# The second norm's weight is multiplied in on VectorE after the gathered rows are transposed

## The chip, the cores and the metric

The kernel runs on one core of one Trainium2 chip. The metric is the device time of one execution in microseconds (us). The kernel before took 1095.0 us as the median of three runs (1093.69 to 1096.15 us).

## The reference, cut to what matters

One decoder layer works on 544 tokens of width 1024: 512 of a prompt and 32 of eight sample sequences.

```
xn = rms_norm(x, mix_norm_g)
h  = x + mixer(xn)                      # three gated branches, three projections, one output projection
hn = rms_norm(h, ffn_norm_g)            # h * rsqrt(mean(h*h) + eps) * ffn_norm_g
group  = argmax(softmax(hn @ w_group + b_group))           # 1 of 4
top 2  of the 8 experts of that group, by hn @ w_router + b_router
y  = h + sum over the 2 experts of gate * (silu(hn @ w_gate_e) * (hn @ w_up_e)) @ w_down_e
out = rms_norm(y, final_norm_g)
```

There are 32 experts with three weight matrices of 1024 x 512 in float32, 2048 KB each, so 6 MB an expert. All of them are read. The change concerns `ffn_norm_g`, the weight of the second norm, 1024 numbers: each row of `hn` is multiplied by it, element by element.

## The kernel before, in words

Everything is float32, and every instruction is placed by hand on one of five queues: SP issues the transfers, TensorE (PE) multiplies and transposes, ScalarE (ACT), VectorE (DVE) and GpSimd (POOL) do the rest. They wait for each other through semaphores. The order of each queue is the order of its text.

**The mixer** fills the time to about 517 us. Its weights come in blocks of 1024 x 256 through two buffers (`wring`, lines 474 to 476); ACT writes the high part of each block (`high_part`, line 885), POOL subtracts it to get the low part (`low_part`, line 1445), and PE multiplies both (lines 587 and 628). At the start SP issues the inputs, 32 tiny pieces of the gating weights (line 437) and eight "late" loads (lines 439 to 450), and only then the third weight block. Near the end of the mixer SP reloads `x` and loads `ffn_row`: `ffn_norm_g` repeated on all 128 partitions (line 473).

**The second norm and the routing** (about 517 to 563 us). The rows of `h` lie in `x`, 128 tokens a chunk, five chunks (the last has 32 rows). PE transposes them (line 770) and multiplies by the router's weights (line 757); those weights were multiplied by `ffn_norm_g` on DVE at the start (line 1118), and each row's scale is applied to the logits later (line 1275), so the routing needs neither the scaled rows nor the weight row. ACT scales the rows into `xn2` (line 1035, one instruction for a chunk, semaphore `h_scaled`). POOL multiplies each chunk of `xn2` by `ffn_row` in place (line 1509, semaphore `xn2_done`), SP stores the chunk to DRAM as `xn2_dram` (lines 494 to 497, semaphore `xn2_stored`). Meanwhile DVE computes the routing from the logits, one small instruction after the other (lines 1289 to 1366), with two exponentials on ACT (lines 1038 and 1040) and three small products on PE (lines 786, 787 and 792). It ends with a table of row numbers, `block_rows`, and the semaphore `routed`.

**The experts.** For each expert, POOL copies a column of row numbers (line 1517) and gathers 64 token rows as 128 half rows of 512 from `xn2_dram` with an indirect transfer (line 1520, `gather`). It waits for `routed` and for all of `xn2_stored` first. PE transposes the half rows into PSUM (`turn_rows`, line 803), DVE copies the 128 x 512 result to SBUF as `xgT` (`take_rows`, line 1372), and PE multiplies by the gate and up matrices (`gate_up`, line 814). ACT applies silu (line 1046), DVE multiplies (`times_up`, line 1378), PE transposes (line 825), ACT copies (line 1052), PE multiplies by the down matrix (`down`, line 835), ACT copies the result out (line 1058), and POOL scatters it (line 1532). PE's order is written out: gate/up of e, transposing of the rows of e+1, transposing of the hidden values of e, down of e.

**The weight stream.** Gate/up matrices have three places, down matrices three; the third place of each is used once, for expert 2. SP's order from 517 us on: gate and up of expert 0, up and down of expert 1 (gate of 1 and down of 0 came earlier), the five stores of `xn2`, down of expert 2 (line 499, into `late_rows`, where `ffn_row` lay), then a wait for all stores and for the first two gathers (lines 500 to 502), gate and up of expert 2, and then for each later expert (`load_expert`, line 506): wait until the gate/up product two experts earlier is done, load gate and up, wait for the down product, load down. `final_row`, the weight of the last norm, lies where `ffn_row` lay; both loads count on `norm_rows_loaded`.

Of the kernel before, what the change touches and what calls it, by code (L numbers as in the profile page):

```python
# [22 lines left out]
P = 128  # L23
D = 1024
# [8 lines left out]
NCH = SEQ // P + 1  # L33
# [5 lines left out]
CAP = 64  # L39
# [10 lines left out]
def chunk_rows(c):  # L50
    return P if c < NCH - 1 else NS
# [47 lines left out]
def build(nc, d, out):  # L99
    ctx = ExitStack()  # L100
    with ctx:
        program(nc, d, out, ctx)


def program(nc, d, out, ctx):
    def sb(name, shape, dt=F32):
        return ctx.enter_context(nc.sbuf_tensor(name, shape, dt))
# [8 lines left out]
    def sem(name):  # L116
        return ctx.enter_context(nc.semaphore(name))
# [22 lines left out]
    gate_of = sb("gate_of", [P, 2, NCH])  # L140
    block_rows = sb("block_rows", [P, 2 * NBLK], I32)
    idx_now = sb("idx_now", [P, 4], I32)
    ovf = sb("ovf", [P, NOVF + 1], I32)
    ps = ctx.enter_context(nc.psum_tensor("ps", [P, 8, 512], F32))

# [22 lines left out]
    late_rows = xx[:, KD * T:]  # L168
# [14 lines left out]
    pool_hist = row_a[:, 0:KW * NSEQ * PH].rearrange("p (q t) -> p q t", t=NSEQ * PH)  # L183
    xT = xx[:, 0:KD * T].rearrange("p (k t) -> p k t", t=T)

    ffn_row = final_row = late_rows[:, 0:D]
    pool_d = mid[:, 0:KW * T].rearrange("p (q t) -> p q t", t=T)
    vn = mid[:, KW * T:KW * T + NCH * W].rearrange("p (c n) -> p c n", n=W)
    merged = mid[:, 0:KD * T].rearrange("p (q t) -> p q t", t=T)
# [10 lines left out]
    xn2 = flat_y[:, 0:NCH * D].rearrange("p (c n) -> p c n", n=D)  # L200
# [19 lines left out]
    xgT = [work[:, SPARE + 4 * D + s * 512:][:, 0:512].rearrange("p (c m) -> p c m", c=4) for s in range(2)]  # L220
# [16 lines left out]
    def halves(v):  # L237
        return v.rearrange("p (b n) -> p b n", b=2)
# [7 lines left out]
    def halves_at(t, q):  # L246

        return t[:, bass.ds(q, 1)].rearrange("p a (b n) -> p (a b) n", b=2)
# [34 lines left out]
    rows_loaded = sem("rows_loaded")  # L283
    late_loaded = sem("late_loaded")
    norm_rows_loaded = sem("norm_rows_loaded")
    high_ready = sem("high_ready")
    low_ready = sem("low_ready")
    step_loaded = sem("step_loaded")
# [31 lines left out]
    conv_high = sem("conv_high")  # L320
    conv_low = sem("conv_low")
    tap_step = sem("tap_step")
    xn2_done = sem("xn2_done")
    rstd_in = sem("rstd_in")
    h_scaled = sem("h_scaled")
    xn2_stored = sem("xn2_stored")
# [14 lines left out]
    xgT_ready = sem("xgT_ready")  # L341
# [75 lines left out]
    def _(sp):  # L417
# [17 lines left out]
        for b in range(NSEQ):  # L435
# [10 lines left out]
            (router_b[:, 0:NG], d["b_group"][0].partition_broadcast(P)),  # L446
            (router_b[:, NG:], d["b_router"][0].partition_broadcast(P)),
        ]
        for dst, src in late:
            sp.dma_start(dst, src).then_inc(late_loaded, 16)  # L450

# [3 lines left out]
        for n in range(2, len(pairs)):  # L455
            if n == FIRST_D1 + 2:

                sp.wait_ge(v_normed, NCH)
                sp.dma_start(out["chunk_v_sample"][0].rearrange("b i c -> (b i) c"), vn[0:NS, NCH - 1]).then_inc(outs_stored, 16)
                sp.wait_ge(act_took, A_G0 + 2)  # L460
                sp.dma_start(out["pool_prompt"][0][0], states[0:PH, 0]).then_inc(states_stored, 16)
                sp.dma_start(out["conv_prompt"][0][0], states[0:CH, 2]).then_inc(states_stored, 16)
                for b in range(NSEQ):
                    r = slice(b * STEP, (b + 1) * STEP)
                    sp.dma_start(out["pool_sample"][0][b, PH - STEP:PH], states[r, 1]).then_inc(states_stored, 16)
                    sp.dma_start(out["conv_sample"][0][b, CH - STEP:CH], states[r, 3]).then_inc(states_stored, 16)
            if n == FIRST_OUT + 2:


                sp.wait_ge(merged_done, KD)  # L470
                sp.dma_start(x[:, 0:4], d["x_prompt"][0].rearrange("(c p) n -> p c n", p=P)).then_inc(x_again, 16)
                sp.dma_start(x[0:NS, 4], d["x_sample"].rearrange("b i n -> (b i) n")).then_inc(x_again, 16)
                sp.dma_start(ffn_row, d["ffn_norm_g"][0].partition_broadcast(P)).then_inc(norm_rows_loaded, 16)
            sp.wait_ge(low_ready, n - 1)
            rows = pairs[n].rearrange("(k p) n -> p k n", p=P)
            sp.dma_start(wring[n % 2][:, 0:rows.shape[1]], rows).then_inc(wring_loaded[n % 2], 16)
# [15 lines left out]
        load_down(1, 1)  # L492

        for c in range(NCH):
            sp.wait_ge(xn2_done, c + 1)
            n = chunk_rows(c)
            sp.dma_start(xn2_dram[c * P:c * P + n], xn2[0:n, c]).then_inc(xn2_stored, 16)

# [35 lines left out]
        for c in (4, 0, 1, 2, 3):  # L534
            n = chunk_rows(c)
            sp.dma_start(y_place(c)[0:n], y_rows[c * P:c * P + n]).then_inc(y_loaded[c], 16)
        for i, c in enumerate(FINAL_ORDER):
            sp.wait_ge(final_done, i + 1)
            n = chunk_rows(c)
# [543 lines left out]
    def _(dve):  # L1083
        v = nc.vector
        n_own = [0]

        def own(instruction):

            n_own[0] += 1
            instruction.then_inc(dve_step, 1)  # L1090
            dve.wait_ge(dve_step, n_own[0])
# [9 lines left out]
        for c in range(NCH):  # L1101
            n = chunk_rows(c)
# [49 lines left out]
        for c in range(NCH):  # L1152
            n = chunk_rows(c)
# [7 lines left out]
        for c in range(NCH):  # L1161
            n = chunk_rows(c)
# [70 lines left out]
        with dve.Fori(0, NJ // 2) as i:  # L1233
            for b in range(4):
                m = halves_at(merged, i * 4 + b)
                t = halves(tmp[b % 2][:, 0:T])
# [12 lines left out]
        for i in range(2):  # L1249
            for c in range(NCH):  # L1250
                n = chunk_rows(c)
# [20 lines left out]
        for c in range(NCH):  # L1272
            n = chunk_rows(c)
# [94 lines left out]
        def take_rows(e, s, turn, free):  # L1368
            dve.wait_ge(xg_turned, e + 1)
            if free is not None:  # L1370
                dve.wait_ge(gu_done, free)
            v.tensor_copy(xgT[s].rearrange("p c m -> p (c m)"), ps[:, s]).then_inc(xgT_ready, 1)  # L1372

        def times_up(e, s, turn, free):
            dve.wait_ge(sig_ready, e + 1)
# [2 lines left out]
            v.tensor_tensor(hid[s], sig[s], ps[:, 2 + s, 256:512], ALU.mult).then_inc(hid_ready, 1)  # L1378

        dve.wait_ge(xn2_stored, 16 * NCH)  # L1380
        take_rows(0, 0, 0, None)
        for e in range(2):
            take_rows(e + 1, 1 - e, e, None if e == 0 else 1)
            times_up(e, e, 0, None)
        with dve.Fori(1, NE // 2 - 1) as i:
            for s in range(2):
                take_rows(2 * i + s + 1, 1 - s, i + s, 2 * i + s)
                times_up(2 * i + s, s, i, 2 * i + s - 1)
# [9 lines left out]


        own(v.memset(stat[:, 95:96], EPS))  # L1400
        dve.wait_ge(norm_rows_loaded, 32)

        def last_sum(c):
            dve.wait_ge(y_loaded[c], 16)
# [22 lines left out]
    def _(pool):  # L1427
        g = nc.gpsimd
# [73 lines left out]
            low_part(s, FIRST_OUT + 2 + s)  # L1502


        pool.wait_ge(norm_rows_loaded, 16)
        for c in range(NCH):
            n = chunk_rows(c)
            pool.wait_ge(h_scaled, c + 1)
            g.tensor_tensor(xn2[0:n, c], xn2[0:n, c], ffn_row[0:n], ALU.mult).then_inc(xn2_done, 1)

        def gather(e, s, turn, free):
# [77 lines left out]
```

## Time and profile before

| what | value |
| --- | --- |
| median of three runs | 1095.0 us (1093.69 to 1096.15) |
| span of the profiled execution, first to last instruction | 1089.4 us |
| own time of the profiled execution | not listed apart from its span; the median lies 5.6 us above the span |
| busy share of the span | PE 79%, PEld 54%, DVE 36%, POOL 30%, ACT 18% |
| read from HBM, written | 256.60 MB, 13.74 MB |

How to read it: an engine's busy share is an average over very different stretches. The page also has a strip that cuts the span into 40 slices of 27.2 us, with busy tenths for each engine, the clock that TensorE was granted, and what the transfers moved. The chain of waits follows the work back from the last instruction: at each step to what released it, or to the instruction before it on its engine. A line number (L1372) is a line of the kernel. SPq is SP's queue of transfers.

### The profile page before, as it was taken

To read this page: it belongs to the slowest core of one execution; us is meant where nothing else is said; L and a number is where in the kernel's file an instruction comes from. 1 tells how busy PE (TensorE), PEld (TensorE's weight loads), DVE (VectorE), ACT (ScalarE), POOL (GpSimd) and SP (SyncE) were. 2 spreads that over 40 slices of the span, in tenths; PEclk is the share of its full clock that TensorE was granted. 3 is DMA by queue.
4 is the path that set the end of the run, shared out by engine and by line. 5 is a ranking of instruction groups with operands and counts; after the bars stand their busy time and mean duration, and the time that the engine had idled before them with its cause. 6 is when DMAs were issued, how large, how long until landed. Compare 5 with 4: busy or idle time off the path is not lost.

```text
span 1089.4 us, 13673 instructions
## 1 busy us (share of the span) xinstructions
PE 859.8 (79%) x5197; PEld 586.5 (54%) x5197; DVE 388.8 (36%) x571; ACT 201.3 (18%) x304; POOL 325.3 (30%) x239
## 2 busy tenths in 40 slices
PE   1999988449999999799429888888788778778860
PEld 1999888449999999799113333222222223223220
DVE  4206999986458454511750000000000000000008
ACT  4323212032212432212400100000000000000003
POOL 2234999025424414411410111111011101111104
PEclk9999989769999999899759999999999999999985
DMA  7423121012223222351939999999999999999935
GB/s 217 143 79 107 47 78 39 1 60 68 97 66 103 63 78 96 102 193 77 387 105 403 372 408 420 420 419 421 420 420 419 421 420 421 420 421 418 421 147 214
DMA packets 73515, 262.26 MB, mean 241 GB/s; under 512 B 8743, under 2 KB 42691, under 8 KB 48352
## 3 DMA queue, kind: packets, MB, share of 16 engines
q1 hardware_dynamic: 68368, 252.96, 59.2%
q0 software_dynamic: 5120, 8.93, 2.2%
q8 instruction: 17, 0.28, 0.1%
q14 instruction: 10, 0.08, 0.0%
HBM read 256.60 MB, written 13.74 MB: 248 GB/s over the span
## 4 chain that ended last, share of the span: by engine, by line
PE 37%; DMA 25%; DVE 19%; issue 11%; POOL 4%; ACT 3%; SPq 1%; DVEq 0%; POOLq 0%; ACTq 0%
DMA gu<-in_w_up_e 24%; PE ps L814 14%; DVE work L1143 11%; PE ps L587 10%; PE ps L628 5%; POOL w_low L1445 4%; PE ps L835 4%; DVE xh L1103 1%; PE ps L561 1%; DVE xh L1414 1%; DMA xh<-in_x_prompt 1%; PE ps L803 1%; DVE xh L1406 1%; PE ps L672 1%; ACT w_high L885 1%
## 5 line engine op out<-in xcount | busy, mean ns | idle before, releaser
L1445 POOL TENSOR_TENSOR w_low<-ring,w_high 128x2048 fp32r<-128x2048 f32 (+1 forms) x38 | 155.5, 4092 | 236.6 <-ACT w_high L885 236.4
L587 PE MATMUL ps<-x_high,w_high 128*128 128x272 f32 x640 | 175.6, 292 | 7.3 <-POOL w_low L1445 7.3
L1372 DVE COPY work<-ps 128x512 f32<-128x512 f32 x32 | 22.1, 692 | 440.8 <-PE ps L803 440.8
L587 PE MATMUL ps<-x_low,w_high 128*128 128x272 f32 x640 | 174.2, 290 | 0.0
L1143 DVE SCALAR_TENSOR_TENSOR work<-slot,param,work 128x512 f32<-128x512 f32 x240 | 162.6, 752 | 1.2 <-DVE work L1200 1.2
L1532 POOL DMA_INDIRECT expert_rows<-xx,idx_now x32 | 32.8, 1025 | 387.0 <-ACT xx L1058 355.4
L587 PE MATMUL ps<-x_high,w_low 128*128 128x272 f32 x640 | 133.8, 291 | 0.0
L814 PE MATMUL ps<-gu,work 128*64 128x512 f32 x512 | 118.4, 617 | 19.4 <-DMA gu<-in_w_up_e 18.5
L814 PE MATMUL ps<-slot,work 128*64 128x512 f32 x480 | 112.9, 625 | 18.7 <-issue 18.0
L587 PEld LDWEIGHTS ps<-x_high,w_high 128*128 128x128 f32 x640 | 121.9, 191 | 8.6 <-issue 4.6
L587 PEld LDWEIGHTS ps<-x_low,w_high 128*128 128x128 f32 x640 | 121.7, 190 | 0.0
L587 PEld LDWEIGHTS ps<-x_high,w_low 128*128 128x128 f32 x640 | 101.0, 190 | 0.0
L814 PEld LDWEIGHTS ps<-gu,work 128*64 128x64 f32 x512 | 38.1, 142 | 98.7 <-issue 97.4
L814 PEld LDWEIGHTS ps<-slot,work 128*64 128x64 f32 x480 | 39.9, 143 | 90.5 <-issue 89.6
L885 ACT CAST w_high<-ring 128x2048 fp32r<-128x2048 f32 (+1 forms) x37 | 60.2, 1627 | 83.8 <-PE ps L628 49.2
L835 PE MATMUL ps<-ring,xx 128*64 128x512 f32 x256 | 65.2, 656 | 7.4 <-ACT xx L1052 7.4
L835 PE MATMUL ps<-slot,xx 128*64 128x512 f32 x240 | 56.5, 614 | 6.9 <-ACT xx L1052 6.9
L1046 ACT ACTIVATE xx<-ps 128x256 f32<-128x256 f32 x32 | 12.3, 384 | 263.2 <-PE ps L814 263.2
L587 PE MATMUL ps<-y_high,w_high 128*128 128x272 f32 x192 | 52.2, 290 | 1.9 <-DVE y_low L1187 1.9
L587 PE MATMUL ps<-y_low,w_high 128*128 128x272 f32 x192 | 51.8, 289 | 0.0
L628 PE MATMUL ps<-w_high,m_high 128*128 128x256 f32 (+1 forms) x160 | 46.0, 287 | 7.3 <-DVE xh L1239 5.1
L628 PE MATMUL ps<-w_low,m_high 128*128 128x256 f32 (+1 forms) x160 | 45.8, 286 | 0.0
(240 smaller groups left out, 1080.0 us busy)
## 6 DMA issues: line engine op xcount, KB each, us to landing
ring<-in_w_down_e SPq DMA_DIRECT2D x16, 2048.0 KB, 22.1
gu<-in_w_gate_e SPq DMA_DIRECT2D x16, 2048.0 KB, 18.0
gu<-in_w_up_e SPq DMA_DIRECT2D x16, 2048.0 KB, 23.3
slot<-in_w_gate_e SPq DMA_DIRECT2D x15, 2048.0 KB, 17.5
slot<-in_w_up_e SPq DMA_DIRECT2D x15, 2048.0 KB, 22.8
slot<-in_w_down_e SPq DMA_DIRECT2D x15, 2048.0 KB, 22.4
ring<-in_w_in SPq DMA_DIRECT2D x22, 1024.0 KB, 5.1
ring<-in_w_out SPq DMA_DIRECT2D x4, 1024.0 KB, 8.2
```

Of the source, the lines that this page charges most:

```text
L561: last = pe.transpose(ps[:, 2 * (k % 4) + c // 4, (c % 4) * P:(c % 4) * P + n], x[0:n, c, k * P:(k + 1) * P], ident[0:n, 0:n])
L587: last = pe.matmul(ps[:, 2 * r + half, 0:HT], w[:, k, c * P:(c + 1) * P], part[:, k, half * HT:(half + 1) * HT], start=(k == 0 and len(par ...
L628: last = pe.matmul(ps[0:n, c, s * 256:(s + 1) * 256], part[:, k, c * P:c * P + n], w[:, k], start=(k == 0 and part is high and w is w_high ...
L672: last = pe.matmul(ps[:, 2 * ((h + 1) % 4), c * P:(c + 1) * P], vn[:, c, h * P:(h + 1) * P], wsT[:, h], start=True, stop=True)
L814: last = pe.matmul(ps[g * CAP:(g + 1) * CAP, 2 + s].rearrange("p (m f) -> p m f", m=2), xgT[s][:, k % 4, (k // 4) * CAP:(k // 4 + 1) * CAP ...
L835: last = pe.matmul(ps[g * CAP:(g + 1) * CAP, 6 + s], hT[s][:, k % 2, (k // 2) * CAP:(k // 2 + 1) * CAP], dn[w][:, k, g * W:(g + 1) * W], s ...
L885: nc.scalar.copy(w_high[s][:, 0:kt], wring[s][:, 0:kt]).then_inc(high_ready, 1)
L1046: nc.scalar.activation(sig[s], ps[:, 2 + s, 0:256], ACT.Silu).then_inc(sig_ready, 1)
L1143: last = v.scalar_tensor_tensor(acc, src, w, acc, ALU.mult, ALU.add)
L1372: v.tensor_copy(xgT[s].rearrange("p c m -> p (c m)"), ps[:, s]).then_inc(xgT_ready, 1)
L1445: g.tensor_tensor(w_low[s][:, 0:kt], wring[s][:, 0:kt], w_high[s][:, 0:kt].bitcast(F32), ALU.subtract).then_inc(low_ready, 1)
L1532: pool.indirect_dma_start(y_dram, bass.IndirectOffsetOnAxis(ap=idx_now[:, 2 + s:3 + s], axis=0), yo[s], None, bounds_check=4 * T - 1, oob_ ...
```

## The change

It removes POOL's five multiplications, the row `ffn_row` with its load, and the semaphore `xn2_done`; SP's stores wait for ACT's scaling instead, so that `xn2_dram` holds rows without the weight. It adds a tile `norm_cols` of 128 x 2 x 4 that holds the weight as it lies after the transposing (a gathered half row h has element 4p + c at partition p, column c), loaded once at the start ahead of the late loads in pieces of four numbers. `take_rows` becomes a multiplication of the transposed rows in PSUM by this tile, repeated over the 64 tokens, in place of the copy. DVE waits once for the load of `norm_cols` ahead of the first `take_rows`, and its last wait on `norm_rows_loaded` is for one load in place of two.

```diff
+    norm_cols = sb("norm_cols", [P, 2, 4])
...
-    ffn_row = final_row = late_rows[:, 0:D]
+    final_row = late_rows[:, 0:D]
...
+        sp.dma_start(norm_cols[:], d["ffn_norm_g"][0].rearrange("(h p c) -> p h c", h=2, c=4)).then_inc(norm_cols_loaded, 16)
         for dst, src in late:
             sp.dma_start(dst, src).then_inc(late_loaded, 16)
...
-                sp.dma_start(ffn_row, d["ffn_norm_g"][0].partition_broadcast(P)).then_inc(norm_rows_loaded, 16)
...
         for c in range(NCH):
-            sp.wait_ge(xn2_done, c + 1)
+            sp.wait_ge(h_scaled, c + 1)
             n = chunk_rows(c)
             sp.dma_start(xn2_dram[c * P:c * P + n], xn2[0:n, c]).then_inc(xn2_stored, 16)
...
-            v.tensor_copy(xgT[s].rearrange("p c m -> p (c m)"), ps[:, s]).then_inc(xgT_ready, 1)
+            v.tensor_tensor(xgT[s].rearrange("p c (h t) -> p c h t", h=2),
+                            ps[:, s].rearrange("p (c h t) -> p c h t", c=4, h=2),
+                            wide(norm_cols[:].rearrange("p h c -> p c h").unsqueeze(3), [P, 4, 2, CAP]),
+                            ALU.mult).then_inc(xgT_ready, 1)
...
         dve.wait_ge(xn2_stored, 16 * NCH)
+        dve.wait_ge(norm_cols_loaded, 16)
...
-        dve.wait_ge(norm_rows_loaded, 32)
+        dve.wait_ge(norm_rows_loaded, 16)
...
-        pool.wait_ge(norm_rows_loaded, 16)
-        for c in range(NCH):
-            n = chunk_rows(c)
-            pool.wait_ge(h_scaled, c + 1)
-            g.tensor_tensor(xn2[0:n, c], xn2[0:n, c], ffn_row[0:n], ALU.mult).then_inc(xn2_done, 1)
```

## Rows read from the trace of the kernel before

**Rows 1.** The page: the strip's transfer rate in 40 slices, the chain's shares by engine.

```profile
GB/s 217 143 79 107 47 78 39 1 60 68 97 66 103 63 78 96 102 193 77 387 105 403 372 408 420 420 419 421 420 420 419 421 420 421 420 421 418 421 147 214
...
PE 37%; DMA 25%; DVE 19%; issue 11%; POOL 4%; ACT 3%; SPq 1%; DVEq 0%; POOLq 0%; ACTq 0%
```

**Rows 2.** Chain of waits in order of time: start us, us, what.

```profile
563.71 2.99 DMA xx<-xn_rows,idx_now
...
568.78 8.83 PE ps L814 x32
...
665.04 6.89 PE ps L814 x32
672.56 22.43 DMA gu<-in_w_up_e
```

**Rows 3.** SP's queue: line, waited for, us in total, times, longest.

```profile
SPq L502 <- DMA xx<-xn_rows,idx_now: 25.5, 1, 25.5
```

**Rows 4.** Timeline, POOL and DVE, from 530 us: start, us, instruction.

```profile
530.27 11.75 POOL L1509 TENSOR_TENSOR work<-work,xx 128x1024 f32<-128x1024 f32 x5 [35.75 <-ACT work L1035]
...
530.63 2.04 DVE L1290 TENSOR_TENSOR work<-work 128x20 f32<-128x20 f32 x1
```

**Rows 5.** Groups by form, 522 to 566 us: instruction, count, busy us, mean ns.

```profile
L1295 DVE TENSOR_TENSOR work<-work 128x160 f32<-128x160 f32 x1 | 2.3, 2346 | 0.0
L1296 DVE TENSOR_SCALAR work<-work 128x160 f32<-128x160 f32 x1 | 2.3, 2261 | 0.0
L1292 DVE SCALAR_TENSOR_TENSOR work<-work,cst 128x20 f32<-128x20 f32 x1 | 2.2, 2219 | 0.0
...
L1294 DVE TENSOR_TENSOR work<-cst,work 128x160 f32<-128x160 f32 x1 | 2.2, 2202 | 0.0
...
L1290 DVE TENSOR_TENSOR work<-work 128x20 f32<-128x20 f32 x1 | 2.0, 2037 | 0.0
...
L1301 DVE TENSOR_TENSOR work<-work 128x160 f32<-128x160 f32 x2 | 0.7, 326 | 0.1
...
L1291 DVE TENSOR_TENSOR work<-work 128x20 f32<-128x20 f32 x1 | 0.2, 166 | 0.0
```

**Rows 6.** Last store of xn2 (L497): ns, start us, landing.

```profile
L497 SPq DMA_DIRECT2D xn_rows<-work x1: 318/318/318, 542.0 to 542.0; - x1
...
DMA to landing us min/median/max: 6.3/6.3/6.3
```

**Rows 7.** Down load of expert 2 (L483), 541 to 544 us: ns, start, landing.

```profile
L483 SPq DMA_DIRECT2D xx<-in_w_down_e x1: 1224/1224/1224, 542.4 to 542.4; - x1
...
DMA to landing us min/median/max: 11.9/11.9/11.9
```

**Rows 8.** All gathers (L1520): ns min/median/max, first and last start, landing.

```profile
L1520 POOL DMA_INDIRECT xx<-xn_rows,idx_now x32: 1023/1046/1264, 563.7 to 1013.7; - x32
...
DMA to landing us min/median/max: 3.0/6.8/8.1
```

**Rows 9.** Three DVE lines with a PSUM input: ns min/median/max, starts, forms.

```profile
L1372 DVE COPY work<-ps x32: 690/692/693, 568.0 to 1034.5; 128x512 f32<-128x512 f32 x32
...
L1170 DVE TENSOR_TENSOR work<-ps,bias_rows x4: 683/692/692, 234.9 to 239.5; 128x512 f32<-128x512 f32 x4
...
L1378 DVE TENSOR_TENSOR xx<-xx,ps x32: 408/410/421, 578.9 to 1049.5; 128x256 f32<-128x256 f32 x32
```

**Rows 10.** Third weight block, its first user, and a late load with its landing.

```profile
L476 SPq DMA_DIRECT2D ring<-in_w_in x1: 442/442/442, 34.7 to 34.7; - x1
...
DMA to landing us min/median/max: 7.2/7.2/7.2
...
49.58 1.90 ACT L885 CAST w_high<-ring 128x2048 fp32r<-128x2048 f32 x1
...
router<-in_w_group SPq DMA_DIRECT2D x1, 16.0 KB, 5.1
```

**Rows 11.** Window of the tail: us, busy by engine, granted clock, DMA share, GB/s.

```profile
1036.00:1042.00 6.00, 5.47 (x19) 1.52 (x19) 0.00 (x0) 0.37 (x1) 0.00 (x0) 0.72 0.78 326
```

More of the change, by code:

```diff
@@ L285, in program @@
     norm_rows_loaded = sem("norm_rows_loaded")
+    norm_cols_loaded = sem("norm_cols_loaded")
     high_ready = sem("high_ready")
@@ L322, in program @@
     tap_step = sem("tap_step")
-    xn2_done = sem("xn2_done")
     rstd_in = sem("rstd_in")
```

## The prediction

> **What bounds the kernel now.** I read the page first. The chain's shares are spread over PE, DMA and DVE [rows 1], so the kernel has several stages with different limits. The strip of transfer rates shows which stage is which: from the 22nd slice on (about 572 us) it stays near 420 GB/s almost to the end, and only three of these slices, at 403, 372 and 408, are lower; the slice before them has 105 [rows 1]. So the expert part is a weight stream at its full rate, preceded by a hole. The question is what the stream waits for in that hole.
>
> The chain in order of time answers it [rows 2]. The hole ends with a gather issued at 563.71 us that lands 2.99 us later. Then PE leads through eight gate/up products, the first at 568.78 and the eighth at 665.04; from 672.56 on the chain goes through the loads. SP's queue gives the other half: it stands 25.5 us at L502, where it waits for the first two gathers before it loads gate and up of expert 2 [rows 3]. Whatever brings the first gather forward therefore brings both PE's start and the stream forward, and everything later depends on these two.
>
> What makes the gather late is the routing on DVE. The timeline shows POOL busy with the five multiplications of L1509 from 530.27 for 11.75 us without a break, 2.35 us each, and DVE starting L1290, a product of 20 numbers a partition, at 530.63 and needing 2.04 us for it [rows 4]. The groups by form show that this is not its own cost: five DVE instructions of that stretch take 2.04 to 2.35 us, while L1291 with the same 20 elements takes 0.166 us and L1301 with the same 160 takes 0.326 us [rows 5]. L1290 ends at 532.67, just where POOL's first multiplication ends (530.27 + 2.35 = 532.62). DVE is held by POOL, about one POOL instruction at a time.
>
> **The change, part by part.** *POOL's five multiplications go.* They give back to DVE, instruction by instruction [rows 5]: L1290 2.037 - 0.166 = 1.871; L1292 2.219 - 0.166 = 2.053; L1294 2.202 - 0.326 = 1.876; L1295 2.346 - 0.326 = 2.020; L1296 2.261 - 0.326 = 1.935. The sum is 9.76 us. L1296 has one tensor input where L1301 has two, so its own time may be shorter than 0.326; no row of its form is undisturbed, and with 0.166 as the other end the sum is 9.92. I take 9.76. All of it lies on the chain, since these instructions follow one another up to `routed`.
>
> *What is late next.* The first gather would be issued at 563.71 - 9.76 = 553.95. It also needs all five stores. The last one was issued at 542.0 and landed 6.3 us later, at 548.3 [rows 6]; with ACT's scaling as its releaser it goes out earlier, so 548.3 is a ceiling and leaves 5.6 us. The down load of expert 2, the last transfer ahead of the gathers, was issued at 542.4 and landed at 554.3 [rows 7]. It follows the stores in SP's queue and moves forward with them; even unmoved it would overlap the new gather by 0.3 us. So nothing that I see takes the place of DVE before the gather, and PE and the weight stream start 9.76 us earlier.
>
> *take_rows becomes a product.* Rows of both kinds exist: the copy from PSUM takes 692 ns for 512 elements, and L1170, a product-like instruction of one PSUM input and one SBUF input repeated along an axis, takes 683 to 692 ns for 512 [rows 9]. I take no difference. The new pattern has one more axis and takes a single number for 64 elements, which no row shows; the lower end is nothing and the upper end, all of it doubled, is 0.69 us a call. It counts only where PE leads, in the first eight experts; later the stream hides it, and if that cover were gone each call would cost what it is longer by.
>
> A rule speaks against this edit. The Trainium skill (VectorE: DVE Perf Modes, "The perf-mode tier table") lists a copy with a PSUM operand at up to twice the base rate and a two-tensor operation at the base rate alone, though the text behind the table puts float32 from PSUM at the base rate for both. By the table a call would double, at most 8 x 0.69 = 5.5 us are given back and the time is 1090.8; by rows 9 it is 1085.2. The trace bears out the text behind the table, since 692 and 692 ns are equal.
>
> *The load of `norm_cols`* is put ahead of eight late loads and of the third weight block on SP's queue. It has 256 pieces of four numbers; the load of the group router has 1024 pieces of that size and lands in 5.1 us [rows 10]. Between nothing and 5.1 us, I take a quarter of it, 1.3. The third block was issued at 34.7, landed 7.2 us later at 41.9, and its user, ACT's cast, started at 49.58 [rows 10]: 7.7 us of cover hide even the upper end. DVE's new wait on it stands in front of all its expert work, but the load is done some 500 us earlier.
>
> *The load of `ffn_row` goes* from SP's queue near 458 us, where PE is busy with products whose blocks had been loaded: I cost it at nothing, bounded below by nothing. SP's waits on ACT instead of POOL and DVE's smaller count cost nothing of their own.
>
> **Sum.** The profiled execution's span is 1089.4 us; 1089.4 - 9.76 = 1079.6. The median of the runs lies 5.6 us above that span, and I keep this for the start and end around it: 1085.2 us, 0.9% faster. The 0.2% (2.2 us) is about what a measurement of this kernel can tell from no change.
>
> **The rivals.**
>
> *A. take_rows runs at half rate* (the table above). It would give back up to 5.5 us: 1090.8. For it: the added axis. Against it: rows 9. Chance 0.04.
>
> *B. The gathers meet traffic.* Alone, the first gather landed in 3.0 us; under the stream the median is 6.8 [rows 8]. If stores and the down load of expert 2 don't finish sooner and the gathers queue behind them, 3.8 us are lost: 1089.0. For it: the overlap of 0.3 us at the ceiling. Against it: every transfer in front goes out earlier than before. Chance 0.06.
>
> *C. The change doesn't do what it says for the time.* The five DVE instructions could be slow because of the transfers at that moment, or the hole could stay because SP is held by something else. Then the time stays at 1095.0. Against it: five excesses, each as long as one POOL instruction. Chance 0.03.
>
> *D. Slower: POOL holds the new take_rows.* It reads `norm_cols` from SBUF, and POOL issues a gather and a scatter for each expert. Were each call held for both, about 1.05 us each [rows 8], eight experts would lose 8 x 2.1 = 16.8 us: 1102.0. It decides from 9.76 / 8 = 1.2 us a call. Against it: L1378 also reads one input from SBUF and one from PSUM in the same loop and never takes more than 421 ns [rows 9]. Chance 0.03. By the Trainium skill (SBUF — State Buffer, "Who interferes with whom") GpSimd's reads hold a VectorE instruction with two SBUF inputs and not one with a single SBUF input outside the faster modes; by that rule D can't happen, and the 421 ns agree.
>
> **How the numbers follow.** The forecast keeps 0.84. Its own range comes from TensorE's clock: the first gate/up product takes 8.83 us and the eighth 6.89 [rows 2], 1.9 us more for one stretch begun at the lower clock, and in the tail the granted clock is 0.72 [rows 11], part at 1.2 and part at 2.4 GHz, just ahead of the last expert. One such stretch more or less on the chain makes 1.9 us, and the shown runs lie 1.3 below to 1.2 above their median. Together that is 1082.4 to 1087.9; up to 1089.2 it takes in B. A, C, D and the forecast's ends are left out, about 2 in 10. Faster by over 0.2%: forecast, A and B, 0.94. Within 0.2%: C, 0.03. Slower: D, 0.03.
>
> **What would show it.** After: L1290 and L1292 near 0.17 us, L1294 to L1296 near 0.33; the first gather issued near 554; L502 waiting about as long less the earlier routing; L1372's successor at 0.69 us; the first load through which the chain goes near 662.8; the tail unchanged in length. The prediction is wrong if the DVE instructions stay long, if the gather lands more than 3 us after its issue, or if the strip shows a new hole while the gather is early.

## The result, and the profile after

The changed kernel takes 1084.56 us as the median of four runs (1074.94 to 1087.03) against 1094.35 us of the kernel before beside it: a ratio of 0.9893, 95% interval 0.9869 to 0.9918. Measured again on another occasion, with six runs, it is 1083.58 us against 1094.24, ratio 0.9898 (0.9879 to 0.9918). The forecast was 1085.2 us, with a range of 1082.4 to 1089.2.

The page of the kernel after has the same shape as before: the chain's shares move by a point at most, and the strip shows the same stream, with a smaller hole ahead of it (compare [rows 1]; slices are 27.0 us now).

```profile
GB/s 218 145 78 88 68 77 22 20 32 96 78 78 78 98 59 78 83 234 78 319 254 403 344 420 420 419 420 421 419 420 419 421 420 420 420 422 419 421 142 212
...
PE 37%; DMA 25%; DVE 18%; issue 11%; POOL 4%; ACT 3%; SPq 1%; DVEq 0%; POOLq 0%; ACTq 0%
```

The difference is in the timeline of DVE in the routing. These are the five instructions of [rows 5], one line number further on; columns are start, us, instruction.

```profile
531.17 0.18 DVE L1291 TENSOR_TENSOR work<-work 128x20 f32<-128x20 f32 x1
...
531.47 0.18 DVE L1293 SCALAR_TENSOR_TENSOR work<-work,cst 128x20 f32<-128x20 f32 x1
...
531.89 0.32 DVE L1295 TENSOR_TENSOR work<-cst,work 128x160 f32<-128x160 f32 x1
532.25 0.32 DVE L1296 TENSOR_TENSOR work<-work 128x160 f32<-128x160 f32 x1
532.61 0.24 DVE L1297 TENSOR_SCALAR work<-work 128x160 f32<-128x160 f32 x1
```

They take 1.24 us together where they took 11.07. The chain in order of time passes this on, piece by piece as in [rows 2]:

```profile
554.43 3.05 DMA xx<-xn_rows,idx_now
...
559.60 8.86 PE ps L815 x32
...
655.83 6.89 PE ps L815 x32
663.35 23.59 DMA gu<-in_w_up_e
...
1033.85 7.10 PE ps L815 x32
```

The gather is issued 9.28 us earlier (554.43 for 563.71), the first gate/up product starts 9.18 earlier, the first load on the chain 9.21. The last gate/up product of the kernel before stood at this line of the same view:

```profile
1041.94 7.10 PE ps L814 x32
```

So from the first gate/up product to the last it is 474.25 us after and 473.16 before: 1.1 us are lost in the weight stream, and 8.1 us of the gain reach the tail. The new take_rows takes what the copy took (compare [rows 9]; the line of the instruction in the view of its source):

```profile
L1373 DVE TENSOR_TENSOR work<-ps,norm_cols x32: 691/692/693, 558.9 to 1026.4; 128x512 f32<-128x512 f32 x32
```

The span is 1081.2 us against 1089.4. This adds up from the starts above: the routing's first instruction (L1290, the reduce ahead of the five) starts 0.54 us later at 530.96, the way from there to the gather is 9.82 shorter, from the gather to the first product 0.10 longer, the stream 1.09 longer, and the tail 0.11 shorter: -8.2 us.

### The profile page after: what moved, and what is told of

The parts are those of the page before. It is cut to its first block, busy times and chain, and to the rows that moved or that the text cites. A ratio compares the mean times of both kernels' runs of the same rounds, so it can differ in the third digit from the quotient of the medians.

```text
span 1081.2 us, 13667 instructions
## 1 busy us (share of the span) xinstructions
PE 857.3 (79%) x5197; PEld 585.3 (54%) x5197; DVE 383.5 (35%) x571; ACT 201.5 (19%) x304; POOL 313.7 (29%) x234
## 4 chain that ended last, share of the span: by engine, by line
PE 37%; DMA 25%; DVE 18%; issue 11%; POOL 4%; ACT 3%; SPq 1%; DVEq 0%; POOLq 0%; ACTq 0%
DMA gu<-in_w_up_e 24%; PE ps L815 14%; DVE work L1144 11%; PE ps L588 10%; PE ps L629 5%; POOL w_low L1450 4%; PE ps L836 4%; DVE xh L1104 1%; PE ps L562 1%; DVE xh L1419 1%; DMA xh<-in_x_prompt 1%; PE ps L804 1%; DVE xh L1411 1%; PE ps L673 1%; ACT w_high L886 1%
## 5 line engine op out<-in xcount | busy, mean ns | idle before, releaser
L1373 DVE TENSOR_TENSOR work<-ps,norm_cols 128x512 f32<-128x512 f32 x32 | 22.1, 692 | 442.0 <-PE ps L804 442.0
L836 PE MATMUL ps<-ring,xx 128*64 128x512 f32 x256 | 61.8, 627 | 7.4 <-ACT xx L1053 7.4
```

Source lines behind the costliest of these rows:

```text
L836: last = pe.matmul(ps[g * CAP:(g + 1) * CAP, 6 + s], hT[s][:, k % 2, (k // 2) * CAP:(k // 2 + 1) * CAP], dn[w][:, k, g * W:(g + 1) * W], s ...
L1373: v.tensor_tensor(xgT[s].rearrange("p c (h t) -> p c h t", h=2), ps[:, s].rearrange("p (c h t) -> p c h t", c=4, h=2), wide(norm_cols[:].r ...
```

## The experiments

All of them are the changed kernel with one edit. Ratios are to the kernel before, measured beside them. The changed kernel again, the products put back, take_rows twice and the copy ran on one chip; the memsets and the last three ran on another, where no run of the changed kernel itself stands beside them.

### The changed kernel again

> The changed kernel again, unchanged, as the level for the runs beside it. Every theory expects about 0.989 of the kernel before (1084 to 1086 us against 1094 to 1095), the first gather issued near 554 us and the five routing instructions of VectorE at 0.17 to 0.33 us each.

Measured: 1083.58 us, ratio 0.9898 (0.9879 to 0.9918); first gather at 555.25 us, the five instructions as above. It is the level for the runs on its chip.

### GpSimd busy at the old place

```diff
+        for c in range(NCH):
+            n = chunk_rows(c)
+            pool.wait_ge(h_scaled, c + 1)
+            own(g.tensor_tensor(flat_y[0:n, NCH * D:(NCH + 1) * D], xn2[0:n, c], xn2[0:n, c], ALU.mult))
```

> The changed kernel, with five GpSimd products of 128 x 1024 put back at the old place, reading the scaled rows and writing to spare memory that nobody reads; the stores don't wait for them. Theory 1 (GpSimd holds VectorE, one product at a time): the five routing instructions take 2.0 to 2.4 us again, the first gather is issued 9 to 10 us later than in the changed kernel, and the time is back at 1094 to 1095 us. Rival (the gain came from the stores going out earlier, or from the load that went): the routing stays short and the time stays at 1084 to 1086 us.

Measured: 1090.57 us, ratio 0.997 (0.9957 to 0.9983), 7.0 us above the changed kernel. Timeline of POOL and DVE:

```profile
530.58 9.76 POOL L1515 TENSOR_TENSOR work<-work 128x1024 f32<-128x1024 f32 x5 [35.66 <-ACT work L1036]
...
531.00 1.51 DVE L1291 TENSOR_TENSOR work<-work 128x20 f32<-128x20 f32 x1
...
532.63 1.85 DVE L1293 SCALAR_TENSOR_TENSOR work<-work,cst 128x20 f32<-128x20 f32 x1
...
534.72 1.87 DVE L1295 TENSOR_TENSOR work<-cst,work 128x160 f32<-128x160 f32 x1
536.62 1.93 DVE L1296 TENSOR_TENSOR work<-work 128x160 f32<-128x160 f32 x1
538.59 1.85 DVE L1297 TENSOR_SCALAR work<-work 128x160 f32<-128x160 f32 x1
```

The numbers I expected were too high, and most of the reason is in the first line: the POOL product put back, with one tile as both inputs and its output elsewhere, takes 9.76 / 5 = 1.95 us, not 2.35, and the five DVE instructions shrink with it, to 1.51 to 1.93 us. Together they take 9.01 us, 7.77 more than in the changed kernel; the way from L1290 to the gather is 31.30 us against 23.48 in the run above, 7.8 longer, and 7.0 reach the end. The stores go out early here and the load of `ffn_row` is gone, so neither of them makes these 7.0 us. The change gained 10.7 us on this chip (1094.24 to 1083.58). Of these, 7.0 come back, and the shorter products hold for 2.0 us less (9.82 - 7.8); the 1.7 us left are within the intervals of the two ratios, about 1.4 us either way here and 2.1 for the changed kernel, and no run puts them down to a cause. The hold is shown, and that its price in the routing follows the length of POOL's product.

### GpSimd busy, but only writing

```diff
+        for c in range(NCH):
+            n = chunk_rows(c)
+            pool.wait_ge(h_scaled, c + 1)
+            for _ in range(3):
+                own(g.memset(flat_y[0:n, NCH * D:(NCH + 1) * D], 0.0))
```

> The changed kernel, with GpSimd kept busy at the old place by fifteen memsets of 128 x 1024 into spare memory: it writes SBUF and reads nothing. Theory 1a (VectorE is held by what GpSimd reads): the four routing instructions with two tensor inputs stay at 0.17 to 0.33 us, at most the one with a single input (tensor_scalar on 160 elements) is held, and the time is 1084 to 1086 us. Theory 1b (any GpSimd instruction on SBUF holds VectorE): these instructions become as long as the memsets, and the first gather is some us later, up to 10 us.

Measured: 1082.49 us, ratio 0.989 (0.986 to 0.992).

The time is 1.5 us below the 1084 to 1086 us that theory 1a gave; the interval overlaps that of the changed kernel.

```profile
530.93 15.08 POOL L1516 MEMSET work<- 128x1024 f32 x15 [35.62 <-ACT work L1036]
...
531.36 0.18 DVE L1291 TENSOR_TENSOR work<-work 128x20 f32<-128x20 f32 x1
...
531.67 0.18 DVE L1293 SCALAR_TENSOR_TENSOR work<-work,cst 128x20 f32<-128x20 f32 x1
...
532.09 0.32 DVE L1295 TENSOR_TENSOR work<-cst,work 128x160 f32<-128x160 f32 x1
532.45 0.32 DVE L1296 TENSOR_TENSOR work<-work 128x160 f32<-128x160 f32 x1
532.80 0.24 DVE L1297 TENSOR_SCALAR work<-work 128x160 f32<-128x160 f32 x1
```

POOL is busy for 15.08 us across the whole stretch, longer than before, and none of the five takes longer than in the changed kernel. For the four with two inputs it is POOL's reading that costs, not that it runs. The Trainium skill (SBUF — State Buffer, "Who interferes with whom") says so of VectorE instructions with two SBUF inputs, and the four lines agree.

Two instructions of this stretch are tensor_scalar, with a single tensor input: L1297 and, farther on, L1314. These are the memsets that run when they start (POOL's timeline in the windows 532.0 to 532.1 and 538.1 to 538.2 us); the last line is from the changed kernel, the others are from this run:

```profile
531.94 0.95 POOL L1516 MEMSET work<- 128x1024 f32 x1
...
538.03 0.95 POOL L1516 MEMSET work<- 128x1024 f32 x1
...
538.26 0.74 DVE L1314 TENSOR_SCALAR work<-work 128x5 f32<-128x5 f32 x1
...
538.06 0.17 DVE L1314 TENSOR_SCALAR work<-work 128x5 f32<-128x5 f32 x1
```

L1297 settles nothing: it starts 0.09 us before a memset ends (531.94 + 0.95 = 532.89). L1314 starts 0.23 us into a memset, takes 0.74 us where it takes 0.17 in the changed kernel, and ends at 539.00, as that memset does (538.98). So a memset can hold such an instruction, as far as one case shows it. The Trainium skill says in the same section that GpSimd and a single-input instruction in one of the faster modes block each other, which would fit; that L1314 ran in such a mode is not shown. The 0.57 us are not on the chain: from L1290 to the gather it is 23.53 us, and 23.47 in the changed kernel.

### take_rows twice

```diff
+            v.tensor_tensor(work[:, SPARE + 4 * D + 1024:].rearrange("p (c h t) -> p c h t", c=4, h=2),
+                            ps[:, s].rearrange("p (c h t) -> p c h t", c=4, h=2),
+                            wide(norm_cols[:].rearrange("p h c -> p c h").unsqueeze(3), [P, 4, 2, CAP]),
+                            ALU.mult)
             v.tensor_tensor(xgT[s].rearrange("p c (h t) -> p c h t", h=2),
```

> The changed kernel with each take_rows done twice, first into spare memory and then where it belongs: 0.6 to 0.7 us more for each of the 32 calls. Theory (a call counts only in the first eight experts, where TensorE leads): at most 4.8 to 5.5 us more than the changed kernel, about 1090 us. Rival 1 (the weight stream hides it everywhere): no difference, 1085 us. Rival 2 (every call counts): 19 to 22 us more, about 1105 us.

Measured: 1086.18 us, ratio 0.9921 (0.9899 to 0.9943), in the median 2.6 us above the changed kernel, with intervals that overlap. That every call counts is excluded; "in the first eight experts" and "hidden everywhere" are not told apart by the times. The chain in order of time says more:

```profile
561.14 8.54 PE ps L815 x32
...
661.29 6.89 PE ps L815 x32
668.82 20.41 DMA gu<-in_w_up_e
```

From the first to the eighth gate/up product it is 100.15 us here, and 96.23 in the changed kernel (559.60 to 655.83), each with one down product at the lower clock (5.35 and 5.29 us where the others take 3.65): seven added calls make 3.9 us, 0.56 each. So they do count on TensorE. But the first load on the chain then lasts 20.41 us, where it is 23.59 in the changed kernel: 3.2 of these 3.9 us had been waited for in the queue anyway. The stream hides most of the added calls. Not all of the rest lies in the first eight experts: this chain leaves the loads twice more, from 783.17 to 853.23 us and from 909.78 to 948.73, for TensorE with added calls in its way, which the changed kernel's does not. From the first gate/up product to the last it is 475.59 us, 0.9 more than in the run above on the same chip (474.68).

### The copy put back, the weight left out

```diff
-            v.tensor_tensor(xgT[s].rearrange("p c (h t) -> p c h t", h=2),
-                            ps[:, s].rearrange("p (c h t) -> p c h t", c=4, h=2),
-                            wide(norm_cols[:].rearrange("p h c -> p c h").unsqueeze(3), [P, 4, 2, CAP]),
-                            ALU.mult).then_inc(xgT_ready, 1)
+            v.tensor_copy(xgT[s].rearrange("p c m -> p (c m)"), ps[:, s]).then_inc(xgT_ready, 1)
```

> The changed kernel with the old copy in take_rows; the second norm's weight is left out of the experts' input altogether. Theory (the product costs what the copy cost, 0.69 us): no difference from the changed kernel, within 0.2%. Rival A (the product is slower): the copy's instruction is shorter than the product's, and the time is up to 5.5 us below the changed kernel.

Measured: 1084.8 us, ratio 0.9913 (0.9892 to 0.9934), not told apart from the changed kernel.

```profile
L1373 DVE COPY work<-ps x32: 691/692/692, 560.3 to 1027.2; 128x512 f32<-128x512 f32 x32
```

Copy and product are equal to a nanosecond, with the repeated single numbers too. The multiplication is free where a copy stood already.

### The last chunk's sum on VectorE

The five chunks' final sums have the same pair: POOL sums the chunk of 32 rows (L1558 and L1559 in the changed kernel) while DVE sums and norms the others. In the run above of the changed kernel again, the timeline of the tail reads:

```profile
1059.49 3.21 POOL L1558 TENSOR_SCALAR slot<-slot,gate_of 32x1024 f32<-32x1024 f32 x1 [9.36 <-issue]
1059.91 2.14 DVE L1411 SCALAR_TENSOR_TENSOR xh<-gu,gate_of,xh 128x1024 f32<-128x1024 f32 x1
...
1062.79 2.77 POOL L1559 TENSOR_TENSOR xh<-xh,slot 32x1024 f32<-32x1024 f32 x1
...
1063.48 3.17 DVE L1419 SCALAR_TENSOR_TENSOR xh<-xh,stat,xx 128x1024 f32<-128x1024 f32 x1
...
1066.57 2.13 DVE L1411 SCALAR_TENSOR_TENSOR xh<-gu,gate_of,xh 128x1024 f32<-128x1024 f32 x1
...
1070.13 3.18 DVE L1419 SCALAR_TENSOR_TENSOR xh<-xh,stat,xx 128x1024 f32<-128x1024 f32 x1
```

The price is not POOL's whole instruction here: beside the tensor_scalar of 3.21 us L1411 is 0.86 us longer than its undisturbed 1.28 and ends first, at 1062.05 against 1062.70, while beside the product of 2.77 us L1419 is 1.89 us longer. The profile's spans of POOL are rough, and no run says why the two differ.

The edit takes the four POOL instructions out and lets DVE do this chunk first, while it waits for chunk 0:

```diff
         def last_sum(c):
+            n = chunk_rows(c)
...
-            v.scalar_tensor_tensor(x[:, c], yr[:, 1], gate_of[:, 1, c:c + 1], x[:, c], ALU.mult, ALU.add).then_inc(summed, 1)
+            v.scalar_tensor_tensor(x[0:n, c], yr[0:n, 1], gate_of[0:n, 1, c:c + 1], x[0:n, c], ALU.mult, ALU.add).then_inc(
+                summed if c < NCH - 1 else pool_summed, 1)
...
+        last_sum(NCH - 1)
         last_sum(0)
...
-        pool.wait_ge(y_loaded[NCH - 1], 16)
-        rows = y_place(NCH - 1)[0:NS].rearrange("p (k n) -> p k n", k=2)
-        for k in range(2):
-            own(g.tensor_scalar(rows[:, k], rows[:, k], gate_of[0:NS, k, NCH - 1:NCH], None, ALU.mult))
-            last = g.tensor_tensor(x[0:NS, NCH - 1], x[0:NS, NCH - 1], rows[:, k], ALU.add)
-            if k == 0:
-                own(last)
-        last.then_inc(pool_summed, 1)
```

> The changed kernel with GpSimd's work at the end (the last chunk's sum) given to VectorE, ahead of chunk 0. Theory 1 (the same hold, in the tail): the sums and norms of chunks 0 to 2 that take 2.06, 3.18, 2.07 and 3.18 us become 1.28 us each, 5.4 us less, and the new two instructions cost nothing to 2.6 us: 2.8 to 5.4 us below the changed kernel, 1078 to 1081 us. Rival (the end is set by the loads or by ScalarE): no difference.

Measured: 1077.86 us, ratio 0.9837 (0.981 to 0.9864); 5.7 below the changed kernel's 1083.58 and 6.7 below its 1084.56, of other occasions, so a little more than the 2.8 to 5.4 us forecast. The next two kernels, measured on the same occasion, differ by the tail's edit alone and lie 4.0 us apart (1084.55 and 1080.6). In the traces, from the last scatter to the start of the last DVE instruction, it is 25.08 us here and 29.80 in the changed kernel again: 4.7 less, within the forecast.

```profile
1053.91 1.27 DVE L1412 SCALAR_TENSOR_TENSOR xh<-slot,gate_of,xh 32x1024 f32<-32x1024 f32 x1 [2.95 <-DMA slot<-expert_rows]
1055.22 1.27 DVE L1413 SCALAR_TENSOR_TENSOR xh<-slot,gate_of,xh 32x1024 f32<-32x1024 f32 x1
1056.42 1.27 DVE L1412 SCALAR_TENSOR_TENSOR xh<-gu,gate_of,xh 128x1024 f32<-128x1024 f32 x1
...
1062.25 1.29 DVE L1421 SCALAR_TENSOR_TENSOR xh<-xh,stat,xx 128x1024 f32<-128x1024 f32 x1
```

The added pair nearly fits into the wait for chunk 0 (its sum starts 8.41 us after that scatter, 8.23 in the changed kernel again), and all the other sums and norms take 1.27 to 1.29 us. The same hold, in another place, with the price read from the rows ahead of the run: this is strong support for the reading of the first part, and the fastest kernel of the study.

### The gate matrix of expert 2 early

```diff
         sp.wait_ge(xn2_stored, 16 * NCH)
+        load_gate_up(2, 2, 0)
         for c in range(2):
             sp.wait_ge(xg_loaded[c], 16)
-        for m in range(2):
-            load_gate_up(2, 2, m)
+        load_gate_up(2, 2, 1)
```

> The changed kernel with the gate matrix of expert 2 loaded as soon as the stores have landed, into the hole ahead of the first gathers; only the up matrix waits for the gathers. Theory S (the start of the weight stream sets the end): 2 MB less remain to be moved after the gathers, at 420 GB/s 5.0 us less, about 1079 us. Theory P (TensorE's start, by the places that its first products free, sets the end): the stream runs dry that much earlier ahead of the loads of expert 3 and the time stays at 1083 to 1086 us.

Measured: 1084.55 us, ratio 0.9911 (0.9889 to 0.9932): no gain, as theory P has it. First SP's transfers in its timeline (start, length, line):

```profile
550.15 0.38 SPq L481 DMA_DIRECT2D work<-in_w_gate_e  x1
561.88 0.37 SPq L481 DMA_DIRECT2D work<-in_w_up_e  x1
571.07 0.37 SPq L481 DMA_DIRECT2D gu<-in_w_gate_e  x1
```

The first gather in its chain of waits (start, length):

```profile
556.19 4.14 DMA xx<-xn_rows,idx_now
```

And one stretch of its windows; the last three columns are granted clock, DMA share and GB/s:

```profile
569.00:571.00 2.00, 2.00 (x11) 0.47 (x7) 0.00 (x0) 0.00 (x0) 0.00 (x0) 1.00 0.03 12
```

The gate matrix goes out at 550.15 into the hole, 2 MB are moved ahead, and then the queues stand still at 569 to 571 us (share 0.03), because the load of expert 3 may only go out when the first gate/up product has freed its place, at 571.07. In the changed kernel again the share of that window is 1.01:

```profile
569.00:571.00 2.00, 1.22 (x8) 0.68 (x8) 0.86 (x2) 0.38 (x1) 0.00 (x0) 1.00 1.01 426
```

And the first gather, now under traffic, lands after 4.14 us instead of 3.05. What sets the pace at the start of the stream is when TensorE frees the first place, and so the first gather.

### Both of the last two

> Both of the edits before it in one kernel: the last chunk's sum on VectorE and the gate matrix of expert 2 early. Theories 1 and P: as with the first edit alone, 1078 to 1081 us. Theories 1 and S: 1073 to 1076 us.

Measured: 1080.6 us, ratio 0.9872 (0.9848 to 0.9896), in the median 2.7 us slower than the tail's edit alone, with intervals that overlap. The first chunk's gather and TensorE's first work after it, from the chain of waits of this kernel:

```profile
555.49 5.44 DMA xx<-xn_rows,idx_now
...
563.05 9.61 PE ps L815 x32
```

The first gather takes 5.44 us to land here, 2.4 longer than in the changed kernel (3.05), and TensorE starts that much later after the gather's issue (7.56 us for 5.17). Loading the gate early is worth nothing here; that it costs is seen in the gather, and not beyond the intervals in the time.

## Why the prediction was right, and where not

**The hold of DVE by POOL: right.** The forecast was 9.76 to 9.92 us; the five instructions became 9.83 us shorter (11.07 to 1.24), and the way from the routing's first instruction to the gather 9.82. L1296's own time, which no row showed, is 0.24 us, between the two ends. The products put back restore the hold at the length of the products; writing alone doesn't hold any of the five.

**What is late next: right, with less room than it looks.** The last store and the down load of expert 2, by the views of their sources between 534.5 and 540 us in the kernel after:

```profile
L498 SPq DMA_DIRECT2D xn_rows<-work x1: 317/317/317, 534.9 to 534.9; - x1
...
DMA to landing us min/median/max: 13.6/13.6/13.6
...
L484 SPq DMA_DIRECT2D xx<-in_w_down_e x1: 427/427/427, 535.2 to 535.2; - x1
...
DMA to landing us min/median/max: 18.1/18.1/18.1
```

I had said that the last store goes out earlier, so that 548.3 is a ceiling. It goes out 7.1 us earlier and lands at 534.9 + 13.6 = 548.5, no earlier at all: it stands in the queue behind the expert loads, and only its wait became longer [rows 6]. The last of these loads lands at 519.3 + 23.8 = 543.1 us, as it did before (518.7 + 24.3 = 543.0); this is the view of its source from 519.1 to 519.9 us after:

```profile
L484 SPq DMA_DIRECT2D slot<-in_w_down_e x1: 534/534/534, 519.3 to 519.3; - x1
...
DMA to landing us min/median/max: 23.8/23.8/23.8
```

The down load lands at 553.3, one microsecond earlier than before [rows 7]. The room ahead of the gather was there all the same: POOL begins to prepare it at 553.25. But the conclusion that the transfers in front move forward with their issue, on which rival B's low chance rested, was wrong; B's own mechanism appears as soon as a load is put into the hole, with 4.14 and 5.44 us to land. One sign that I had named didn't come either: SP's wait for the first two gathers did not shorten by the earlier routing (25.5 us before [rows 3]), since SP comes to it 8.0 us earlier too.

```profile
SPq L503 <- DMA xx<-xn_rows,idx_now: 24.2, 1, 24.2
```

**take_rows at no cost: right** (692 ns both ways), so rivals A and D are out: the largest of the 32 new calls takes 693 ns beside POOL's gathers and scatters. **The eight experts as the measure of its cost: too high.** Doubling the call lengthens TensorE's first part by 3.9 us, but most of it is taken out of the stream's queue, so rival D's 16.8 us and A's 5.5 us were upper ends; later the stream did not hide every call, as the chain of that run shows.

**The load of `norm_cols` at no cost: right.** It is issued in 0.39 us at 25.41 and lands after 2.7 us, twice the 1.3 that I took and within the 5.1. SP comes to the third weight block at 34.75 where it was 34.73 [rows 10]: the load ahead of `norm_cols` was through its issue 0.4 us sooner in that run, and a later load, of `router_b`, is through its issue at 32.7 in both. So the trace shows no cost, and does not say which of the two hid it.

**The sum: right by two errors that offset each other.** The predicted span was 1079.6 and the profiled one is 1081.2: 0.54 us of a later start and 1.09 in the stream. In the other direction, I took the median's 5.6 us above the span as the time around an execution. The runs of the kernel after list both: 1083.14 us for a span of 1081.2, so 1.9 lies around it. The profiled execution before was one of the shorter ones, and 3.7 of the 5.6 us were the difference between executions. Against the median the term came out as 3.4 us (1084.56 - 1081.2), since the profiled execution after lies below its median as well, by 1.4. What I called the time around an execution was mostly something else, and a sum against one execution's span has that spread as its error. Between medians the term drops out: 9.76 us were forecast, and the medians differ by 9.8 us (1094.35 to 1084.56) and by 10.7 on the other occasion, while the two profiled spans differ by 8.2. The ends of the forecast's own range don't follow from their terms: 1.9 with 1.3 and 1.2 gives 1082.0 to 1088.3, not 1082.4 to 1087.9; the median lies inside either.

**Rival C: excluded** by the products put back. What stays open: why single runs of the changed kernel differ by up to 12 us (1074.94 to 1087.03), and the 1.09 us of the stream, where two gate/up products at the lower clock (8.80 us, in both kernels, in other places) are on the chain. No run separates these.

## What to carry to other kernels

When a VectorE instruction takes far longer than one of the same form nearby, look which GpSimd instruction begins before it and ends with it: here, five VectorE instructions with their inputs in SBUF were each held for the rest of a GpSimd product, and a chain of small operations paid 9.8 us for work that was not on the chain. Not everything beside a product was held: the reduces took 0.17 us, and so did a two-input instruction that began as one product ended. In the tail the price was less than GpSimd's whole instruction. A per-channel factor cost nothing here, where a transposed tile was copied out of PSUM anyway (692 ns either way). And read what the freed time runs into next before shortening further: here the last store lands 4.8 us ahead of the new gather's preparation, and moving loads into the hole in front of it gained nothing.

## What the runs showed that I had not expected

GpSimd's memsets ran for 15.08 us beside the same five VectorE instructions and lengthened none of them, while products of 1.95 and 2.35 us each held them to their end; yet one tensor_scalar of five numbers, begun inside a memset, lasted to that memset's end (0.74 us for 0.17). And a store issued 7.1 us earlier landed at the same time, with the last load ahead of it landing at 543 us in both kernels.
